# The weighted sum of a group's second expert row: from VectorE to GpSimd, in more stages

## What is computed

```python
def block(args):
    xb, eb, gb = args
    a = jax.nn.gelu(jnp.einsum('tkd,td->tk', u_tab[eb], xb), approximate=False)
    return jnp.einsum('tk,tkd->td', gb * a, v_tab[eb])
```

## Time and profile before

| | |
|---|---|
| median of 3 runs | 5304.95 us (5303.41 to 5306.64) |
| the profiled execution | 5302.89 us, its span 5301.1 us |
| busy, share of the span | TensorE 74%, VectorE 54%, ScalarE 32%, GpSimd 27% |
| mean granted TensorE clock | 0.855 of full speed |

### The profile page before, as it was taken

The page is one execution under the profiler, slowest core; times in us unless marked ns, Lnnn a source line. Parts: engine busy times, 40 slices in busy tenths (PEclk is TensorE's granted clock), DMA queues, the critical chain, the costliest instruction groups (busy, mean ns, idle before and its releaser), DMA issues.

```text
span 5301.1 us, 61468 instructions
## 1 busy us (share of the span) xinstructions
PE 3919.9 (74%) x21152; PEld 2352.9 (44%) x21152; DVE 2878.4 (54%) x6732; ACT 1709.3 (32%) x4654; POOL 1457.7 (27%) x1295
## 2 busy tenths in 40 slices
PE   5998687889976886676576667897667997655555
PEld 3676554656743553333232335676234664211111
DVE  1313767666568446765455443334676457844454
ACT  1210237342533534333322322221235343322222
POOL 0000022222222333333343341000332233345453
PEclk8899899889988998787788788798788998777677
DMA  6346477778998999999999995125987999899998
GB/s 252 143 159 244 158 272 272 277 279 315 407 371 324 384 420 384 400 393 381 383 420 392 409 420 221 65 95 214 383 358 262 350 391 381 329 421 421 402 421 352
DMA packets 265337, 1712.53 MB, mean 323 GB/s; under 512 B 37600, under 2 KB 39232, under 8 KB 77632
## 3 DMA queue, kind: packets, MB, share of 16 engines
q0 software_dynamic: 184320, 1342.26, 63.1%
q1 hardware_dynamic: 80704, 366.33, 18.5%
HBM read 1690.46 MB, written 17.92 MB: 322 GB/s over the span
## 4 chain that ended last, share of the span: by engine, by line
PE 39%; DMA 27%; DVE 18%; ACT 5%; issue 4%; POOL 3%; DVEq 2%; ACTq 2%; SPq 0%; PEldq 0%; POOLq 0%; PEld 0%
PE psum L540 25%; DMA arena<-in_uv,arena 24%; PE psum L930 9%; DVE arena L2318 7%; POOL arena L1313 3%; DVE arena L2221 1%; DVE arena L2214 1%; PE psum L485 1%; DVE arena L2215 1%; DMA arena<-in_norm_g 1%; DMA arena<-in_w_ada 1%; ACT arena L1410 1%; PE psum L729 1%; PE psum L728 1%; PE psum L557 1%
## 5 line engine op out<-in xcount | busy, mean ns | idle before, releaser
L1313 POOL DMA_INDIRECT arena<-in_uv,arena x1280 | 1453.8, 1136 | 3806.1 <-PE psum L930 2204.7
L2318 DVE CUSTOM_DVE_ANT_0 arena<-arena 128x1024 f32<-128x1024 f32 x1280 | 1551.3, 1225 | 1202.2 <-DMA arena<-in_uv,arena 1142.7
L930 PE MATMUL psum<-arena 64*64 64x512 f32 x9576 | 1476.0, 743 | 913.7 <-ACTq L1701 824.1
L540 PE MATMUL psum<-arena 128*128 128x256 f32 (+2 forms) x8480 | 1971.0, 390 | 155.3 <-DVEq L1720 104.1
L540 PEld LDWEIGHTS psum<-arena 128*128 128x128 f32 (+1 forms) x8480 | 1625.0, 196 | 599.4 <-issue 182.4
L930 PEld LDWEIGHTS psum<-arena 64*64 64x64 f32 x9576 | 360.6, 156 | 1793.4 <-ACTq L1701 1155.4
L1694 ACT ACTIVATE arena<-arena 128x2 f32<-128x2 f32 x640 | 131.0, 205 | 1600.2 <-DVEq L2320 1585.3
L1700 ACT ACTIVATE arena<-arena 128x64 f32<-128x64 f32 x1197 | 356.2, 341 | 45.3 <-issue 1.0
L1697 ACT ACTIVATE arena<-arena 128x1 f32<-128x1 f32 x1280 | 307.4, 287 | 46.9 <-issue 3.1
L485 PE MATMUL psum<-arena 128*128 128x128 f32 (+1 forms) x680 | 117.1, 323 | 167.2 <-DVE arena L1781 45.3
L1694 ACT ACT_TABLE_LOAD x158 | 202.7, 1283 | 41.0 <-DVEq L2320 37.3
(11 more groups left out here) (207 smaller groups left out, 2449.3 us busy)
## 6 DMA issues: line engine op xcount, KB each, us to landing
arena<-in_w_in SPq DMA_DIRECT2D x92, 1024.0 KB, 7.5
arena<-in_w_mix SPq DMA_DIRECT2D x88, 768.0 KB, 8.2
arena<-in_w_ada SPq DMA_DIRECT2D x32, 1536.0 KB, 11.0
arena<-in_w_wq SPq DMA_DIRECT2D x40, 1152.0 KB, 9.4
arena<-in_w_mix SPq DMA_DIRECT2D x24, 1024.0 KB, 5.4
arena<-in_w_wo SPq DMA_DIRECT2D x20, 1024.0 KB, 8.6
arena<-in_uv,arena POOLq DMA_INDIRECT x1280, 10.9
arena<-ada_rows SPq DMA_DIRECT2D x15, 512.0 KB, 5.6
```

Of the source, the lines that this page charges most:

```text
L540: ins = mm(out, a, b, start=(i == 0), stop=(i == last))
L930: ins = mm(psum[o, r_ * 512:r_ * 512 + 512], DIAG[rows, c, :], RING[rows, sl, D + half * 512:D + (half + 1) * 512], start=first, stop=last ...
L1313: pool.indirect_dma_start(RING[:, sl, :], None, io["uv"], bass.IndirectOffsetOnAxis(IDX[:, t, h * TOPK + k:h * TOPK + k + 1], 0)).then_inc ...
L2318: V_.tensor_tensor_reduce(out=RING[:, sl, 0:D], in0=RING[:, sl, 0:D], in1=XT[:, u % 2, :], scale=1.0, scalar=0.0, op0=ALU.mult, op1=ALU.ad ...
```

## The change

GpSimd makes the sum of the second slots in place of VectorE. In its queue it stands behind the two gathers of group g and is for group g-3 (`LAG_POOL`); it waits for the weights (`diag`) and for its own last add. It takes two instructions, `tensor_scalar` into the slot itself and `tensor_tensor` into `XP`, with a drain between them. The three lines of VectorE that made it are gone.

More groups are marked. Layer 0's `ml` and `da` and layer 1's `da` join `ADDED_STAGES`, and all steps of `merge` count. That makes 136 marked groups: 4 to 59 of unit 0 (25 before), 4 to 39 of unit 1 (30 before), 40 to 51 and 56 to 59 of unit 6 (7 before) and 4 to 31 of unit 7 (21 before). For the 53 new ones TensorE sums one slot in place of two, and ScalarE makes one `DIAG` in place of two.

```diff
-LAG_ACT, LAG_PE, LAG_TAIL = 1, 2, 3
+LAG_ACT, LAG_PE, LAG_TAIL, LAG_POOL = 1, 2, 3, 3
...
         for stage, row in rows:
-            for n, count in enumerate(row):
-                out += [stage if stage[0] != "merge" or n < 24 else None] * count
+            out += [stage] * sum(row)
...
-ADDED_STAGES = [(kind, 0, (1, 2)) for kind in ("qkv", "mlp", "mc")] + [("merge", 0, (1,)), ("q", 1, (2,)), ("mc", 1, (2,)), ("merge", 1, (2,))]
+ADDED_STAGES = [(kind, 0, (1, 2)) for kind in ("qkv", "mlp", "mc")] + [("ml", 0, (1, 2)), ("da", 0, (1, 2)), ("merge", 0, (1,)), ("q", 1, (2,)), ("da", 1, (2,)), ("mc", 1, (2,)), ("merge", 1, (2,))]
...
                         pool.indirect_dma_start(RING[:, sl, :], None, io["uv"], bass.IndirectOffsetOnAxis(IDX[:, t, h * TOPK + k:h * TOPK + k + 1], 0)
                                                 ).then_inc(gathered[sl], 16)
+                    j = u * GROUPS + g - LAG_POOL
+                    if j >= 0 and BESIDE[j]:
+                        _, sl, c, _, _ = slots(u, g - LAG_POOL)[1]
+                        pool.wait_ge(s("diag"), j + 1)
+                        if N_BESIDE[j] > 1:
+                            pool.wait_ge(s("beside"), N_BESIDE[j] - 1)
+                        if not any(BESIDE[u * GROUPS:j]):
+                            if u:
+                                pool.wait_ge(s("added"), u)
+                            pool.tensor_scalar(out=XP, in0=RING[:, sl, D:2 * D], scalar1=WGT[:, c:c + 1], scalar2=None, op0=ALU.mult).then_inc(s("beside"), 1)
+                        else:
+                            pool.tensor_scalar(out=RING[:, sl, D:2 * D], in0=RING[:, sl, D:2 * D], scalar1=WGT[:, c:c + 1], scalar2=None, op0=ALU.mult)
+                            pool.drain()
+                            pool.tensor_tensor(out=XP, in0=RING[:, sl, D:2 * D], in1=XP, op=ALU.add).then_inc(s("beside"), 1)
...
-                late = PSEQ[i - LAG_PE] if i >= LAG_PE else None
-                if late is not None and BESIDE[late[0] * GROUPS + late[1]]:
-                    j = late[0] * GROUPS + late[1]
-                    n, sl, c, h, k = slots(*late)[1]
-                    dve.wait_ge(s("diag"), j + 1)
-                    if not any(BESIDE[late[0] * GROUPS:j]):
-                        TSC(XP, RING[:, sl, D:2 * D], WGT[:, c:c + 1], None, ALU.mult).then_inc(s("beside"), 1)
-                    else:
-                        STT(XP, RING[:, sl, D:2 * D], WGT[:, c:c + 1], XP, ALU.mult, ALU.add).then_inc(s("beside"), 1)
```

## The result

The changed kernel takes 5936.3 us (median of 4 runs, 5922.9 to 5952.1), the kernel before 5305.8: a ratio of 1.119, interval 1.1173 to 1.1208. The direction was forecast, the size was not: +631 us in place of +34, outside the range. The profiled execution has a span of 5925.9 us against 5301.1.

A forecast was written before the change was run, and what follows sets the result against it. Marked stages were taken as bound by TensorE (merge), ScalarE and VectorE (attention), the gather ring (convolution) and TensorE alternating with VectorE (scan). 33 + 5 + 0 + 4 - 8 = +34 on 5302.9 gave 5337 us, range 5262 to 5405.

The forecast's parts named there:

- What bounds the kernel, where it is marked: Marked stages: TensorE in merge, ScalarE and VectorE in attention, gather ring in convolution, TensorE and VectorE alternating in scan.
- went round the ring: Convolution stage: the chain runs gather, landing, dots, add on VectorE, next gather.
- What an add costs on GpSimd: GpSimd's queue: multiply, 0.1 us drain and addition take 3.6 us, from 2.4 to 6.3.
- One-input form: GpSimd's 128x1024 tensor_scalar, extrapolated from 626 ns at 512 columns and 288 at 128: 1.08 us.
- Its length is hidden as long as GpSimd keeps up: GpSimd's queue: gathers behind the add aren't delayed, since a group takes 6.1 us there against merge's 7.2.
- Rival two: GpSimd becomes the bound through a slow two-input instruction: +88 in the merges, +50 in attention, 5400 to 5440 us; 12%.
- VectorE is held in turn: Shared SBUF port: VectorE's instructions with two SBUF operands wait for GpSimd's add, up to its full 3.5 us.
- Attention's step: Attention: dots held by GpSimd's add lengthen a step by 1.5 us, 6.87 to 8.4; +33 us in all.
- Scan: Scan: half of TensorE's double sums gives -7, dots held at the port +12; together +5, from -10 to +20.
- Closing steps: Merge's closing steps: some 9 newly marked groups on TensorE's chain save 0.86 us each, -8 us.
- First stages: Convolution and projections (layer 0's qkv, mlp, mc): relief of VectorE and port holds cancel, 0, from -20 to +20.
- Rival one: VectorE isn't held: attention 0, scan gives 7, closing steps 8, first stages up to 20; -35, 5268 us; 26%.

The follow-up runs named there:

- e7: Changed kernel, but ScalarE multiplies and GpSimd only adds, without drain; marked are the groups of before and merge's closing steps: 5276.3 us, ratio 0.9961.
- e10: Changed kernel with 136 marked groups and no sum of second slots; GpSimd clears one column of XP instead: 5265.2 us, ratio 0.9928.
- e2: Kernel before, adds still on VectorE, with attention and scan added to the marked stages: 5340.5 us, ratio 1.0066.
- e1: Changed kernel with a semaphore in place of the drain between GpSimd's multiply and add: 5441.5 us, ratio 1.0258.
- e9: Changed kernel with all 136 marked groups, but ScalarE multiplies and GpSimd makes one plain add: 5332.2 us, ratio 1.0057.
- e11: e10 with TensorE summing the first slot twice in the marked groups of layer 0's scan: 5257.0 us, ratio 0.9915.

## Why the prediction was wrong

**What bounds the kernel, where it is marked:** right in the main. Unit 1's merge stays at TensorE's pace when the queue is short (136.6 us in e7 and e10), and the convolution stage went round the ring. Two readings were too simple. Attention has some slack on VectorE, since e2 puts an add of 1.3 us into a step and the step grows by 0.65. And I took unit 7's merge for a copy of unit 1's, while its chain went round the ring.

**What an add costs on GpSimd:** this step failed, in two terms. "With 0.1 us for the drain (estimate, an issue gap's size)": a drain left 4.1 us (median) between the two instructions, and the add lies outside of the bounds I gave (from 2.4 to 6.3 us; it took 10.3 on average). I priced it by an empty pipeline, and asked neither what stands ahead of it in the queue nor what the engine counts as unfinished. It stands behind two gathers. The trace of before had no drain on GpSimd between gathers, so no row could price it; the honest upper bound was the gather's landing, 7.7 us in the earlier trace rows and 10.9 in the median of that trace, since that is the longest work in flight on that queue. With the 7.7 a group is 1.3 + 7.7 + 2.4 + 0.8 = 12.2 us against 7.2 to 8.8, and 136 groups give an estimate of +460 to +680 us, a case that was missing among the rivals. "One-input form: 1.08 us": it took 2.87, an extrapolation from another operation. The two-input form was right (2.4; 2.34 unheld).

**Its length is hidden as long as GpSimd keeps up:** the condition was right and decided it. I put the queue at 6.1 us a group against 7.2; it was 13.1, and 8.8 without the drain. Rival two, "GpSimd becomes the bound", is what happened, with the chance of 12% and a price of +88 in the merges from a slow `tensor_tensor`. The mechanism and the place were right; the cause and the size (+204 in the two merges) weren't.

**VectorE is held in turn:** right, and no longer an assumption (e1, e9), but not where I had it. The rule cited from the Trainium skill (SBUF — State Buffer, "SBUF: two separate sides") agrees with the holds by GpSimd's addition (17 of 17 of L1882 in e1). For the multiply the trace shows a hold too, but only over the first part of its shown span. Of the 107 dots that start during a multiply of e1, 30 do so in its first 0.96 us: 24 of these take 1.25 to 2.07 us, and in the other six the multiply is the one that waits (4.05 to 4.29 us). Of the 77 later ones 74 take 1.21 to 1.23, and in the other three the multiply waits too (3.83 to 4.26 us). All stretched dots end 0.65 us before the multiply's shown end, and the 128x2 instruction 1.71 us before it, 1.15 after its start. So the multiply shuts VectorE out for some 1.15 us of its 2.87; what GpSimd does in the rest stays open.

Attention's step was forecast at 8.4 us and is 8.48 in e1. That is luck in part. My sum had the dots held in attention, and in layer 0's none is; L1882 is (1.99 us for 1.02), and so is the 128x2 instruction, L1862 in e1 (1.54 for 0.17), which my sum doesn't have, and in it the multiply's shown span is longer than I took. In the kernel after the hold is buried: VectorE has time, and it is the dot that holds the addition (3.24 us for 2.34, since both start at the same landing).

**Scan:** I took half of TensorE's group sums as a gain of 7 us. The marks lose some 10 to 15 there (e10 against e11 and e7), through the clock. **Closing steps:** -8 forecast, nothing seen. **First stages:** 0 forecast; the queue made it +16 in the convolution even without a drain (e1). (34 of the 83 adds stand in these stages, not 33.)

**Rival one**, nothing held and nothing queued, gave 5268 us. e10, which builds just that case, took 5265. The total is right by luck, its parts are not: attention gave 5 us where I had 0, the scan lost 9 where I had a gain of 7, and unit 7's merge gave 10.5 where I had nothing.

## What to carry to other kernels

Before a tensor instruction goes into a queue that issues gathers, price everything in its dependency, the drain first: put it behind a DMA and it can cost a landing; a semaphore on the instruction itself cost 0.1 us. Sum the queue per unit of work and hold it against the pace of each stage, and split a two-step operation so that the slow queue gets only the step it is good at (here ScalarE's 1.13 us multiply in place of GpSimd's 2.87 gave a version faster than both). Taking matmuls from a stage in which TensorE already has idle time (about a fifth of the scan) can lengthen it.

## What the runs showed that I had not expected

- A drain on GpSimd waits for the landing of the gather ahead of it: 0.22 us after it in 93 of 98, and +207 us for 83 bare drains, which end 0.10 us after the start of the dot that the landing releases in 66 of 68.
- A 128x1024 fp32 `tensor_scalar` multiply on GpSimd takes 2.85 us with a constant and 2.87 with a factor by partition, a copy of the same size 1.13, an addition 2.34.
- GpSimd's multiply holds VectorE for some 1.15 us of its shown 2.87; its addition, to the end.
- VectorE's 128x2 `tensor_scalar`, 0.17 us alone, takes 1.3 to 2.6 us in most attention steps when GpSimd's additions or multiplies are near.
- Half the group sums less in the scan (e7 to e10): granted clock 0.95 to 0.72, matmuls 302 to 403 ns, the stage 15 us longer; with the work given back (e11) 0.85, 322 ns and 10 us of it regained.
